# A grouped mixture-of-experts loop: gate matmuls ahead of the up matmuls, each product in its own PSUM bank

## The reference

```
hg  = einsum('td,edf->tef', t, w_gate)      # per expert 1024 -> 512
hu  = einsum('td,edf->tef', t, w_up)        # per expert 1024 -> 512
act = silu(hg) * hu * comb[:, :, None]
out = einsum('tef,efd->td', act, w_down)    # per expert 512 -> 1024
```

## Time and profile before

| | us |
|---|---|
| median of 3 runs (range) | 1263.42 (1262.17 to 1265.58) |
| profiled execution, its own time | 1261.68 |
| its span, first to last instruction | 1260.0 |
| PE busy | 1001.1 (79%) |
| DVE busy | 416.3 (33%) |
| ACT busy | 235.3 (19%) |
| POOL busy | 190.4 (15%) |
| mean granted PE clock | 0.918 |

### The profile page before, as it was taken

How to read it: one execution, slowest core, us unless ns; L and a number is a source line. 1 busy time by engine, 2 the same in 40 slices (tenths; PEclk the granted TensorE clock), 3 DMA queues, 4 the chain that set the end, 5 groups by cost and what they waited for, 6 DMA issues and landing times.

```text
span 1260.0 us, 23997 instructions
## 1 busy us (share of the span) xinstructions
PE 1001.1 (79%) x9435; PEld 555.0 (44%) x9435; DVE 416.3 (33%) x1146; ACT 235.3 (19%) x469; POOL 190.4 (15%) x383
## 2 busy tenths in 40 slices
PE   0899999789779886797399999898977999674830
PEld 0444446554435543454155554444443555342510
DVE  0220014875612121122443434544551222110207
ACT  0401002331411211211241111110141212110202
POOL 1200000200032221222120000001012222111231
PEclk9899999899789998999699998899978999887975
DMA  9985442867489999999995231342646769999973
GB/s 321 383 286 182 152 141 93 319 234 323 178 306 392 403 396 407 397 406 386 395 378 203 76 134 34 133 199 87 257 184 208 297 227 396 407 399 415 390 283 132
DMA packets 79884, 344.60 MB, mean 273 GB/s; under 512 B 9206, under 2 KB 9673, under 8 KB 67532
## 3 DMA queue, kind: packets, MB, share of 16 engines
q1 hardware_dynamic: 57108, 289.30, 59.5%
q0 software_dynamic: 14672, 43.36, 9.9%
q10 hardware_dynamic: 8040, 11.01, 2.6%
HBM read 320.02 MB, written 23.63 MB: 273 GB/s over the span
## 4 chain that ended last, share of the span: by engine, by line
PE 56%; DMA 18%; DVE 12%; ACT 4%; issue 3%; another core or an unknown queue 2%; SPq 2%; POOL 1%; POOLq 0%; ACTq 0%; DVEq 0%
PE bank L885 12%; PE bank L678 11%; PE bank L951 10%; DMA ring<-in_moe_w_up_dram 7%; PE bank L892 7%; PE bank L804 7%; DMA arena<-in_moe_w_down_dram 4%; DMA ring<-in_ada_w_dram 2%; DMA slot_rows<-arena,idx 2%; DMA ring<-in_moe_w_down_dram 2%; PE bank L623 1%; DMA arena<-slot_rows,idx 1%; SPq L1470 1%; PE bank L1025 1%
## 5 line engine op out<-in xcount | busy, mean ns | idle before, releaser
L885 PE MATMUL bank<-ring,arena 128*32 128x256 f32 x2304 | 143.5, 405 | 38.6 <-DMA ring<-in_moe_w_up_dram 37.1
L678 PE MATMUL bank<-ring,arena 128*128 128x512 f32 x336 | 144.9, 593 | 1.0 <-ACT arena L1085 1.0
L885 PE MATMUL bank<-arena 128*32 128x256 f32 x1984 | 116.0, 387 | 19.9 <-DMA arena<-in_moe_w_up_dram 19.9
L1437 DVE TENSOR_TENSOR arena<-arena,bank 128x64 f32<-128x64 f32 x136 | 27.4, 201 | 305.1 <-ACT arena L1323 305.1
L951 PE MATMUL bank<-arena,ring 128*128 128x384 f32 x384 | 124.6, 487 | 0.0
L885 PEld LDWEIGHTS bank<-ring,arena 128*32 128x32 f32 x2304 | 77.9, 117 | 98.7 <-issue 55.7
L892 PE MATMUL bank<-ring,arena 128*32 128x256 f32 x1536 | 95.5, 390 | 28.0 <-DVE arena L1439 24.6
L678 PEld LDWEIGHTS bank<-ring,arena 128*128 128x128 f32 x336 | 63.6, 190 | 80.5 <-issue 79.3
L951 PEld LDWEIGHTS bank<-arena,ring 128*128 128x128 f32 x384 | 72.7, 190 | 51.7 <-issue 1.6
L885 PEld LDWEIGHTS bank<-arena 128*32 128x32 f32 x1984 | 65.0, 112 | 66.2 <-issue 27.9
L804 PE MATMUL bank<-ring,arena 128*128 128x512 f32 x192 | 83.2, 593 | 1.3 <-DVE arena L1972 1.3
(11 more groups left out here) (342 smaller groups left out, 1062.1 us busy)
## 6 DMA issues: line engine op xcount, KB each, us to landing
ring<-in_ada_w_dram SPq DMA_DIRECT2D x24, 2048.0 KB, 17.9
ring<-in_moe_w_down_dram SPq DMA_DIRECT2D x22, 2048.0 KB, 27.4
ring<-in_moe_w_gate_dram SPq DMA_DIRECT2D x16, 2048.0 KB, 28.6
ring<-in_moe_w_up_dram SPq DMA_DIRECT2D x16, 2048.0 KB, 34.1
arena<-in_moe_w_gate_dram SPq DMA_DIRECT2D x16, 2048.0 KB, 34.5
arena<-in_moe_w_up_dram SPq DMA_DIRECT2D x16, 2048.0 KB, 39.9
arena<-in_moe_w_down_dram SPq DMA_DIRECT2D x10, 2048.0 KB, 39.3
ring<-in_ev_w_in_dram SPq DMA_DIRECT2D x7, 2048.0 KB, 14.8
```

The lines of the kernel that those rows point to most:

```text
L678: last = pe.matmul(bank[3 * (c % 2) + t], hT[:, k, t * P:(t + 1) * P], slot8(n)[:, k, :], start=k == 0, stop=k == KT - 1)
L885: last = pe.matmul(bank[1][q * BLK:(q + 1) * BLK, 0:HALF], slot_inT[:, k, :], both[:, :, k, q * P:(q + 1) * P], start=k == 0, stop=k == KT ...
L1437: dve.tensor_tensor(act_rows[:, two, :], silu_g[:, two, :], up, ALU.mult).then_inc(S["gated"], 1)
```

## The change

Gate and up no longer share a matmul. `gate_or_up` runs all 32 gate matmuls of a block (128 moving columns each, into `bank[1]`), then all 32 up matmuls (into `bank[3]`), and each group raises `gu_mm` by one. PE waits for the gate matrix only before the expert's loop, and for the up matrix inside it, between the two groups. ACT's silu waits for the gate group; DVE's product waits for silu and for the up group. On SP the gate of place p waits for the gate group of place p-4, and the up of place p has a wait of its own, for the up group of place p-4, with the read of the table that belongs to it. `pair_of` is gone.

```
-            def gate_and_up(s, k):
-                both = pair_of(s)
-                for q in range(4):
-                    last = pe.matmul(bank[1][q * BLK:(q + 1) * BLK, 0:HALF], slot_inT[:, k, :],
-                                     both[:, :, k, q * P:(q + 1) * P], start=k == 0, stop=k == KT - 1)
-                return last
+            def gate_or_up(s, j):
+                for k in range(KT):
+                    for q in range(4):
+                        last = pe.matmul(bank[1 + 2 * j][q * BLK:(q + 1) * BLK, 0:P], slot_inT[:, k, :],
+                                         slot8(s + j)[:, k, q * P:(q + 1) * P], start=k == 0, stop=k == KT - 1)
+                last.then_inc(S["gu_mm"], 1)
...
                 pe.wait_ge(S["rowT"], b + 1)
-                for k in range(KT):
-                    last = gate_and_up(s, k)
-                last.then_inc(S["gu_mm"], 1)
+                gate_or_up(s, 0)
+                pe.wait_ge(*full(s + 1))
+                gate_or_up(s, 1)
                 rows_to_channels()
...
+            pe.sem_inc(S["gu_mm"], 1)
...
-                for j in range(2):
-                    pe.wait_ge(*full(n + j))
+                pe.wait_ge(*full(n))
...
-            for name in ("gu_mm", "rowT_mm", "down_mm"):
-                pe.sem_inc(S[name], 1)
+            for name, last in (("gu_mm", 2), ("rowT_mm", 1), ("down_mm", 1)):
+                pe.sem_inc(S[name], last)
...
-                    act.wait_ge(S["gu_mm"], pair * 2 + (odd + 1))
+                    act.wait_ge(S["gu_mm"], pair * 4 + (2 * odd + 2))
...
-                up = bank[1][:, P:2 * P].rearrange("p (r f) -> p f r", f=FT)[:, 2 * half:2 * half + 2, :]
+                up = bank[3][:, 0:P].rearrange("p (r f) -> p f r", f=FT)[:, 2 * half:2 * half + 2, :]
...
                     dve.wait_ge(S["silu"], pair * 2 + (odd + 1))
+                    dve.wait_ge(S["gu_mm"], pair * 4 + (2 * odd + 3))
...
-                    sp.wait_ge(MS[layer]["gu_mm"], ends)
+                    sp.wait_ge(MS[layer]["gu_mm"], ends * 2 + j)
...
-                        elif j == 0:
-                            expert_through(layer, place - len(PAIR_SLOTS), 0)
+                        else:
+                            expert_through(layer, place - len(PAIR_SLOTS), j)
```

## The result

| | before | after |
|---|---|---|
| median of 14 runs each (range), us | 1263.08 (1260.5 to 1266.62) | 1270.03 (1267.4 to 1275.8) |
| ratio, with its 95% interval | | 1.0058 (1.0042 to 1.0074) |
| profiled execution, its own time, us | 1261.68 | 1274.87 |
| its span, us | 1260.0 | 1273.2 |
| a second profiled execution of each, its own time, us | 1263.75 | 1270.51 |

The change costs some 7 us where 4.1 us of gain were forecast. The first profiled execution of the kernel after is near the slow end of its 14 runs, and that of before near the fast end. So sizes are taken from the second pair where it matters; it differs by 6.8 us, as the medians do.

A forecast was written before the change was run, and what follows sets the result against it. DMA bounds layer 0; layer 1's end is the weight stream's restart plus fixed transfers. 3.0 + 1.4 - 0.3 = 4.1 us gained: 1257.6 profiled, median 1259.3, range 1257.0 to 1265.5.

The forecast's parts named there:

- Code: Expert's body grows from some 200 to 328 PE instructions; 11 instruction transfers of the last stretch become 18, costing 0.3 us.
- the restart: Layer 1: SP's weight issues resume at 1034.38 us after a wait for down_mm; forecast to move to 1031.4.
- Rival 3: Longer loop body doesn't stay with PE, so back jumps wait for transfers: 8.5 to 17 us less 4.1, slower; chance 0.12.
- Matmuls: Gate and up: 128 half-width records take 3.65 us as 64 did, at 0.109 us per gap.
- Rival 2: Short matmuls run slower in a long stream, 0.123 us a gap, giving 1263.5 us; chance 0.12.
- Silu: Silu runs beside the up group, saving 0.30 us per block; ten blocks before layer 1's restart give 3.0 us.
- the cover: Silu, after ACT's table load in every second block, ends before up does: 980.74 against 980.77 us.
- The last block: Layer 1's last expert: down starts at 1211.5 instead of 1216.07; end 4.4 us earlier, 1.4 on top of the 3.0.
- rival 1: Half clock at the last down group takes 1.5 us of the gain, leaving 2.6, so 1260.8 us; chance 0.14.
- Layer 0: Last down group is released by its matrix with DMA full, so a faster block gains 0.
- SP: Each up transfer's added table read and wait cost 0 beside the backlog; without that cover 0.8 us once.

The follow-up runs named there:

- the old number of instructions: Gate and up apart in layer 1 only, 16 matmuls of 256 columns per group, layer 1's experts computing something else; 1259.04 us, ratio 0.9968 against the kernel before.
- layer 1 apart: Kernel before with gate and up apart in layer 1 only, layer 0 as before; 1265.55 us, ratio 1.0025 against the kernel before.
- the straight code: Kernel before plus 320 short matmuls (1280 instructions) behind each layer's experts, results unused; 1289.8 us in one run.
- both waits in front: Kernel after with PE's gate and up weight waits together again ahead of the expert's loop; 1272.21 us, ratio 1.0069 against the kernel before.
- the instructions doubled: Kernel before with only its gate and up matmuls cut in two, all waits as before; 1277.96 us, ratio 1.0134 against the kernel before.

## Why the prediction was wrong

**The step that failed is *Code*.** It said: 11 instruction transfers become 18, the cost is spread over the engines, "I take 0.3". The count was right (17 in the 182 us behind the restart, 64 instead of 48 in all). The price was read off the wrong side: I asked what the transfers cost the DMA engines, not how soon PE needs them. With waits and loop control the old body has, by an estimate from the code, some 212 instructions in a block of 6.3 us, a transfer of 256 instructions every 7.6 us. The new one has about 340 in 6.05 us, one every 4.6 us. Where the DMA share between them was 0.93 or more, no two transfers of PE's code began less than 5.6 us apart in any trace of this case. So the old code just got through and the new one doesn't, where PE goes through an expert's first block with the weights at hand; repeats need no code. In place of 0.3 the runs show, in layer 1 before the restart, 0.7 and 2.7 us lost in two holes and 1.7 us more at half clock behind the second in the first profile, and 1.1 and 1.9 us in the same two holes in the second. That turns the 3.0 us of gain up to the restart into losses of 3.9 and 2.6 us.

The Trainium skill ("Runtime: NRT & Kernel Launch", Instruction fetch mechanics) calls the cost of crossing such a 16 KiB block "mostly hidden". The runs agree for the old body and for short matmuls beside an idle DMA system, and disagree for dense code beside a full one, by up to 3.3 us a hole.

**Rival 3 had the right resource and the wrong mechanism.** It made the back jumps pay. In the profile after, four of the six back jumps of the place with seven blocks lie between 1015.4 and 1050.4 us, with no instruction transfer, and the period there is 6.05 to 6.4 us. The longer body stays with PE; what is paid for is its first passage. So 0.12 for slower was too low, for a reason that stood in the rows: PE's rate of use was never set against the spacing of the transfers.

**Matmuls: right.** 0.109 us a gap holds over 128 records: (3.68 - 0.27)/31 is 0.110. Rival 2 falls.

**Silu: right in size, but the cover was thinner than taken.** With the old number of instructions it gives 0.29 to 0.31 us in eight of ten blocks. In the kernel after it gives 0.27 in every second block. In the others ACT's table load ends too late whenever the two stores ahead of it take over a microsecond to issue, which they did in the first profile in four of six cases (up to 1.44 us, in the second up to 1.87). There the gain is 0.2 us at most, or turns into a loss of 0.3. The first profile has it so: 7.0 us late at layer 1's second down group, 6.3 at the sixth, 11.1 at the eighth and 10.9 at the restart. Outside the stretch with the holes that is 0.9 us gained, not 3.0. Why the stores take longer to issue is not shown. The DMA share in these windows had risen from 0.11 and 0.14 to 0.40 and 0.46, partly because the blocks had moved against the transfers.

**The last block: right in kind, about half in size.** The group waits for its matrix, as forecast. From the restart to it the prediction had 1.6 us of gain (4.6 less 3.0); the change gains 0.8 to 1.0, and the form with the old number of instructions in layer 1 2.1. In the second profile it runs at full clock. In the first, rival 1 happened too, and was dearer than the 1.5 us that it was given. The chain of waits:

```profile
1225.96 3.67 PE bank L886 x32
...
1230.77 5.17 DMA slot_rows<-arena
...
1236.16 0.20 POOL small L575
```

The group takes 3.67 us, and its store is now issued after POOL's first LayerNorm loads have started, and takes 5.17 us; with the group at full clock it took 1.71 (layer 1 apart). From the down group to POOL's step 10.2 us pass instead of the 5.5 of the earlier trace rows.

**Layer 0: 0 failed as well**, by 4.6 us (ratio 1.0040). It was true that the matrix sets the last down group, and that the block can't move it much. Overlooked was that this group is on the chain, and everything that disturbs it: half clock after a longer idle time, or missing code. In the second pair 3.1 of the 4.3 us up to the first gather are there, 2.0 in the group itself and 0.9 in the store. The other 1.2 us, by which the group starts late, is no more than two executions of one kernel differ.

**SP: right.** In the form with the old number of instructions in layer 1 the added read shows, with gate and up issued 1.1 us apart instead of 0.4, and the kernel gains what was forecast all the same.

No kernel that computes the reference came out under the kernel before. The version of 1259.04 us needs a layout that has gate apart in 256 columns with four column groups, and I found none.

## What to carry to other kernels

Before splitting instructions, count them per microsecond of straight code and set that against the spacing of the instruction queue's transfers where DMA is full; repeats of a loop of this size need no transfer, its first passage does, and a share of 0.3% on that queue says nothing about waiting. Holes in the middle of a group whose operands are all there, put down to "issue", with a transfer on the instruction queue (q8) ending 1.2 to 1.7 us before PE goes on, are the sign. Look at the granted clock behind such a hole as well: in some traces it fell to about half, which cost as much again as a small hole. And where a wait that ends late shields a chain's last group, the group's own length still counts in full.

## What the runs showed of the hardware

- PE goes on 1.2 to 1.7 us after an instruction transfer of 16 KB (about 1.1 us of one DMA engine) has ended, at nearly all holes of over 0.5 us inside a group in the traces of six kernels (the small holes of the straight code apart).
- Two such transfers on one queue (q8) begin 5.6 us apart or more wherever the DMA share between them was 0.93 or over, in 13 traces, and 3.4 to 4.1 us apart in the closest pairs at shares of 0.02 to 0.3. From 1264 to 1273 us of the straight code, at a share of 0.03, PE was never held up.
- A body of about 340 PE instructions repeats without being loaded again.
- Matmuls of 32 stationary and 128 moving columns in four column groups run at 128 records in 3.68 us, 29 ns a record with a weight load for each.
- After holes of 2.31, 2.35 and 2.76 us PE's granted clock was 0.50 to 0.60 in the 2.4 to 3.7 us that followed (after, layer 1 apart, both waits in front). It was 1.00 after the hole of 1.50 us in the second profile of after, and after one of 2.28 us with the instructions doubled; what decides between the two is not shown.
